# A two-layer diffusion step: four slices of a modulation sum move from TensorE to VectorE, and VectorE's sums get a new timetable

## What is computed

```python
def trunk_layer(l, x, cond, w_ada, b_ada, norm_pre, norm_post, w_in, w_out, ...):
    mod = jax.nn.silu(cond) @ w_ada[l] + b_ada[l]
    shift, scale, gate = jnp.split(mod[:, None, :], 3, axis=-1)
    h = rmsnorm(x, norm_pre[l]) * (1 + scale) + shift
    proj = h @ w_in[l]
    ...
    x = x + gate * rmsnorm(o @ w_out[l], norm_post[l])
    return x, k, v

for l in range(DEPTH):          # DEPTH = 2
    xp, kp, vp = trunk_layer(l, xp, c_ctx, ...)   # 128 context tokens
    xs, _, _ = trunk_layer(l, xs, c, ...)         # 256 latent tokens
```

## Time and profile before

| what | value |
|---|---|
| median of 3 runs | 1183.94 us (1182.51 to 1185.13) |
| the profiled execution: its own time | 1183.69 us |
| its span, first to last instruction | 1181.6 us |
| mean granted TensorE clock | 0.991 |
| PE busy | 1126.5 us, 95% |
| DVE busy | 715.6 us, 61% |

### The profile page before, as it was taken

How to read it: one execution, slowest core, us unless ns; L and a number is a source line. 1 busy time by engine, 2 the same in 40 slices (tenths; PEclk the granted TensorE clock), 3 DMA queues, 4 the chain that set the end, 5 groups by cost and what they waited for, 6 DMA issues and landing times.

```text
span 1181.6 us, 13864 instructions
## 1 busy us (share of the span) xinstructions
PE 1126.5 (95%) x5404; PEld 876.4 (74%) x5404; DVE 715.6 (61%) x985; ACT 421.4 (36%) x660; POOL 50.9 (4%) x98
## 2 busy tenths in 40 slices
PE   2999999999999999999999699999999999999996
PEld 1556667887787877788776588888878887878874
DVE  3445455788788785598873653567656764343335
ACT  4223234333455342233333762223323323243332
POOL 1000010000000001001101000000000000000000
PEclk9999999999999999999999899999999999999998
DMA  9999984565576567657767343455444654433413
GB/s 301 359 325 295 325 276 151 207 221 186 200 248 215 197 240 289 216 181 242 242 213 292 115 136 124 143 195 180 157 154 152 214 196 161 142 99 115 143 36 107
DMA packets 117857, 235.99 MB, mean 200 GB/s; under 512 B 5472, under 2 KB 42368, under 8 KB 114720
## 3 DMA queue, kind: packets, MB, share of 16 engines
q1 hardware_dynamic: 105776, 190.86, 47.7%
q0 software_dynamic: 11440, 41.08, 10.7%
q10 hardware_dynamic: 576, 3.16, 0.7%
HBM read 231.40 MB, written 3.67 MB: 199 GB/s over the span
## 4 chain that ended last, share of the span: by engine, by line
PE 81%; DVE 5%; DMA 5%; ACT 4%; issue 3%; SPq 2%; DVEq 0%; ACTq 0%
PE bank L814 23%; PE bank L816 23%; PE bank L815 23%; DMA raw_first<-in_w_ada 4%; DVE w_lo L1243 2%; PE bank L940 1%; SPq L615 1%; PE bank L752 1%; ACT w_hi L1022 1%; ACT silu L1087 1%; DVE x L1300 1%; PE bank L838 1%; PE bank L923 1%; PE bank L985 1%; PE bank L890 1%
## 5 line engine op out<-in xcount | busy, mean ns | idle before, releaser
L814 PE MATMUL bank<-w_hi,h_op 128*128 128x512 f32 x1128 | 464.7, 412 | 3.1 <-DVE w_lo L1243 2.6
L816 PE MATMUL bank<-w_hi,h_op 128*128 128x512 f32 x1128 | 443.8, 393 | 0.0
L815 PE MATMUL bank<-w_lo,h_op 128*128 128x512 f32 x1128 | 442.3, 392 | 0.0
L1243 DVE TENSOR_TENSOR w_lo<-raw,w_hi 128x1024 fp32r<-128x1024 f32 x224 | 273.1, 1220 | 182.8 <-ACT w_hi L1022 182.6
L1022 ACT ACTIVATE w_hi<-raw 128x1024 fp32r<-128x1024 f32 x224 | 234.2, 1053 | 214.0 <-PE bank L816 211.0
L814 PEld LDWEIGHTS bank<-w_hi,h_op 128*128 128x128 f32 x1128 | 213.2, 189 | 79.9 <-issue 35.3
L816 PEld LDWEIGHTS bank<-w_hi,h_op 128*128 128x128 f32 x1128 | 212.7, 189 | 46.9
L815 PEld LDWEIGHTS bank<-w_lo,h_op 128*128 128x128 f32 x1128 | 213.6, 189 | 39.8 <-issue 0.7
L1424 DVE SCALAR_TENSOR_TENSOR wide<-wide_raw,cond,wide 128x1024 f32<-128x1024 f32 x120 | 151.9, 1275 | 15.2 <-DMA wide_raw<-in_w_ada 15.1
L814 PE MATMUL bank<-w_hi,o_low 128*128 128x512 f32 x192 | 75.9, 396 | 0.0
L816 PE MATMUL bank<-w_hi,o_low 128*128 128x512 f32 x192 | 74.9, 390 | 0.0
(11 more groups left out here) (192 smaller groups left out, 797.3 us busy)
## 6 DMA issues: line engine op xcount, KB each, us to landing
raw<-in_w_in SPq DMA_DIRECT2D x68, 1024.0 KB, 6.1
raw_first<-in_w_ada SPq DMA_DIRECT2D x64, 512.0 KB, 7.6
raw<-in_w_ada SPq DMA_DIRECT2D x32, 1024.0 KB, 5.3
wide_raw<-in_w_ada POOLq DMA_DIRECT2D x64, 512.0 KB, 4.3
raw<-in_w_out SPq DMA_DIRECT2D x32, 1024.0 KB, 5.1
raw<-in_w_in SPq DMA_DIRECT2D x24, 512.0 KB, 6.8
x<-in_x_sample SPq DMA_DIRECT2D x2, 1024.0 KB, 9.7
x<-in_x_sample ACTq DMA_DIRECT2D x2, 1024.0 KB, 10.1
```

The source lines that it names most:

```text
L814: pe.matmul(out, operand(layer, kind, 0, k, t), hi, start=k == begin, stop=False)
L815: pe.matmul(out, operand(layer, kind, 0, k, t), lo, start=False, stop=False)
L816: last = pe.matmul(out, operand(layer, kind, 1, k, t), hi, start=False, stop=k == end)
L1243: dve.tensor_tensor(w_lo[:, half % WRING, :, :].rearrange("p k n -> p (k n)"), src, hi, ALU.subtract)\
```

## The change

Of the scale's 16 slices the first twelve stay on PE (six pairs, the last at step 123). The last four become 16 wide sums of DVE with four 512 KB load pairs of POOL, and a fold of their own, whose DVE part adds to `rows`. The gate's sums run at 11 steps for ten (steps 58 to 127, fold at 130), the scale's at one a step (131 to 146, fold at 149), the shift's at 9 steps for ten (150 to 206, fold at 209). The transpose of the scale's rows (`cols`) moves from step 165 to 168. POOL requests the scale's first two half slices ahead of its wait for the end of attention and of the DFT's constants.

```diff
-WIDE = [(GATE_BLOCK[0], FIRST, 10, 12, 10), (SHIFT_BLOCK, FIRST + 5, 13, 11, 10)]
+SCALE_ADA = 12
+
+WIDE = [(GATE_BLOCK[0], 0, FIRST, 10, 11, 10), (SCALE_BLOCK, SCALE_ADA, FIRST + 5, 3, 10, 10),
+        (SHIFT_BLOCK, 0, FIRST + 6, 6, 9, 10)]
...
-    pairs = [(m, k) for m in range(3) if m not in WIDE_BLOCKS for k in range(0, KT, 2)]
-    for n, (m, k) in enumerate(pairs):
-        put(FIRST, 5 + 14 * n, "ada", m, k, 2)
-    for m, c, s, step, per in WIDE:
-        for k in range(KT):
+    for n, k in enumerate(range(0, SCALE_ADA, 2)):
+        put(FIRST, 5 + 14 * n, "ada", SCALE_BLOCK, k, 2)
+    for m, k0, c, s, step, per in WIDE:
+        for k in range(k0, KT):
             for j in range(4):
-                put(c, s + step * (4 * k + j) // per, "wide_sum", m, k, j // 2, j % 2)
-        put(c, s + step * 4 * KT // per + 2, "wide_fold", m)
+                put(c, s + step * (4 * (k - k0) + j) // per, "wide_sum", m, k, j // 2, j % 2)
+        put(c, s + step * 4 * (KT - k0) // per + 2, "wide_fold", m)
...
-    put(10, 5, "cols", SCALE_BLOCK)
+    put(10, 8, "cols", SCALE_BLOCK)
...
             load_bias(GATE_BLOCK[0])
             load_wide(GATE_BLOCK[0])
+            load_wide(SCALE_BLOCK, 0, 2)
 
             wait_full(pool, "pv", len(units) - 1)
             pool.dma_start(dft_sb[:, :], dft).then_inc(dft_in, 16)
             load_weight(1)
             load_bias(SHIFT_BLOCK)
+            load_wide(SCALE_BLOCK, 2)
             load_wide(SHIFT_BLOCK)
...
+                    if m == SCALE_BLOCK:
+
+                        wait_free(dve, *ada_entry[m, SCALE_ADA - 1])
+                        other = rows
+                    else:
+                        dve.wait_ge(bias_in, 16 * (BIAS_ORDER.index(m) + 1))
...
+                    freed(dve.tensor_tensor(dst[:, :], side_bank(e)[:, :], other[:, :], ALU.add), e)
```

More of the change, by code:

```diff
@@ L81 @@
 FIRST = 3
-WIDE = [(GATE_BLOCK[0], FIRST, 10, 12, 10), (SHIFT_BLOCK, FIRST + 5, 13, 11, 10)]
+SCALE_ADA = 12
+WIDE = [(GATE_BLOCK[0], 0, FIRST, 10, 11, 10), (SCALE_BLOCK, SCALE_ADA, FIRST + 5, 3, 10, 10),
+        (SHIFT_BLOCK, 0, FIRST + 6, 6, 9, 10)]
 WIDE_BLOCKS = [w[0] for w in WIDE]
+WIDE_FROM = {w[0]: w[1] for w in WIDE}
+WIDE_LOADS = [(m, k, half) for m in WIDE_BLOCKS for k in range(WIDE_FROM[m], KT) for half in range(2)]
+NTH_WIDE = {x: n // 2 for n, x in enumerate(WIDE_LOADS)}
 BIAS_ORDER = [SCALE_BLOCK, GATE_BLOCK[0], SHIFT_BLOCK, GATE_BLOCK[1]]
@@ L550, in first_drain @@
         def first_drain(m):
-            return ("wide_fold", m) if m in WIDE_BLOCKS else ada_entry[m, 0]
+            return ada_entry[m, 0] if (m, 0) in ada_entry else ("wide_fold", m)
         def half_ahead(p):
@@ L673, in load_bias, with load_wide @@
                 pool.dma_start(bias_rows[:, :], ada_rows[m]).then_inc(bias_in, 16)
-            def load_wide(m):
+            def load_wide(m, first=0, last=2 * KT):
                 layer, third = BLOCKS[m]
-                for i in range(2 * KT):
+                k0 = WIDE_FROM[m]
+                for i in range(first, min(last, 2 * (KT - k0))):
                     if i >= 2:
@@ L683, in load_wide @@
                     else:
-                        pool.wait_ge(wide_summed[WIDE_BLOCKS[WIDE_BLOCKS.index(m) - 1]], 4 * KT - 2 + 2 * i)
-                    k, col = i // 2, third * D + LANES * (i % 2)
+                        prev = WIDE_BLOCKS[WIDE_BLOCKS.index(m) - 1]
+                        pool.wait_ge(wide_summed[prev], 4 * (KT - WIDE_FROM[prev]) - 2 + 2 * i)
+                    k, col = k0 + i // 2, third * D + LANES * (i % 2)
                     pool.dma_start(wide_raw[:, i % 2, :], w_ada[layer, k * P:(k + 1) * P, col:col + LANES])\
@@ L854, in side_product @@
                     pe.wait_ge(fold_in, 16)
-                    pe.wait_ge(wide_summed[e[1]], 4 * KT)
+                    pe.wait_ge(wide_summed[e[1]], 4 * (KT - WIDE_FROM[e[1]]))
                     for c_ in range(2):
@@ L872, in side_product @@
                     else:
-                        wait_free(pe, *(("wide_fold", e[1]) if e[1] in WIDE_BLOCKS else ada_entry[e[1], KT - 1]))
+                        wait_free(pe, "wide_fold", e[1])
                     for i in range(4):
@@ L1407, in part @@
                     m, k, half, c_ = e[1:]
-                    n = 4 * k + 2 * half + c_
+                    n = 4 * (k - WIDE_FROM[m]) + 2 * half + c_
                     cols = slice(LANES * half, LANES * (half + 1))
                     src = wide_raw[:, half, :]
-                    dve.wait_ge(wide_in[half], 16 * (KT * WIDE_BLOCKS.index(m) + k + 1))
+                    dve.wait_ge(wide_in[half], 16 * (NTH_WIDE[m, k, half] + 1))
                     if n == 0:
@@ L1430, in part @@
                     wait_full(dve, *e)
-                    dve.wait_ge(bias_in, 16 * (BIAS_ORDER.index(m) + 1))
-                    wait_full(dve, *{0: ("first_cols", len(STAGES) - 1), 2: ("cols", SCALE_BLOCK)}[m])
-                    freed(dve.tensor_tensor(dst[:, :], side_bank(e)[:, :], bias_rows[:, :], ALU.add), e)
+                    if m == SCALE_BLOCK:
[3 more added lines that the diff above has]
+                        dve.wait_ge(bias_in, 16 * (BIAS_ORDER.index(m) + 1))
+                        wait_full(dve, *{0: ("first_cols", len(STAGES) - 1), 2: ("cols", SCALE_BLOCK)}[m])
+                        other = bias_rows
+                    freed(dve.tensor_tensor(dst[:, :], side_bank(e)[:, :], other[:, :], ALU.add), e)
                     wait_free(dve, *e)
```

2 lines of the change are left out of this document (1 added, 1 removed).

## The result

The changed kernel is slower. Its median is 1189.51 us (1187.65 to 1191.04, four runs) against 1183.72 us (1182.51 to 1185.13) for the kernel before, run beside it. The ratio is 1.0045, with a 95% interval of 1.0032 to 1.0059. The predicted 1183.2 us is missed and so is the range, which ended at 1188.0. The profiled execution took 1187.65 us, the lowest of the four, with a span of 1185.9 us; all times within the trace are from that execution.

A forecast was written before the change was run, and what follows sets the result against it. The prediction took PE as the bound, with DVE close behind and its sums dependent on buffer return. It summed -2.04 - 1.08 + 0.7 + 1.9 = -0.5 us from 1183.69 to 1183.2 us, range 1180.3 to 1188.0.

The forecast's parts named there:

- pairs and fold: PE's side products: two scale pairs go, one fold comes, the other two folds only move; -2.04 us.
- the waits at 131 and 133: PE's waits for DVE's splits behind the transposes of these steps vanish; -1.08 us, ends 0 and -1.08.
- The fourth rival: The pairs were hidden, removing them saves nothing and the rest cancels: 1183.7 us; chance 0.03.
- the gate's pace: Attention stretch: the gate's faster sums fit into DVE's idle time; taken 0, upper end +6 us.
- the third rival: The gate's pace makes attention late, PE waiting before step 125, up to +6 us: 1189; chance 0.03.
- the scale's sums: Steps 131 to 146: buffer cycles 1.5 us late, DVE's margin taking about half; +0.7 us, ends 0 and +2.5.
- the shift's sums: Steps 150 to 206: buffers return slightly late at the faster pace; +1.9 us, ends 0 and +5.
- one sign of being wrong: Mean landing differing from 4.9 us by more than 0.4, or a wait in none of the named places.
- my own formula: Shift's buffer cycle: mean pair 3.04, request 0.29, landing 4.9, so 8.2 us against 7.65 that PE gives.
- margin that DVE wins back, 1 to 2 us: Shift's stretch: part of the buffers' 1.5 to 5 us lack goes into margin DVE regains where it does not wait.
- The second: Rival: DVE waits for transfers every cycle, PE for splits, steps 176 to 206: 1187.6 us; chance 0.22.
- The first rival: Buffers return in time, landing about 4.2 us; only PE's gain and the two waits count, -3.12: 1180.6; chance 0.26.

The follow-up runs named there:

- e1: The kernel before with only the gate's sums at the new pace, 11 steps for ten, fold at step 130: 1183.76 us.
- e3: The changed kernel with the shift's first three slices left out and its sums back at the old pace, 11 steps for ten: 1182.83 us.
- e4: The changed kernel with four buffers instead of two for the shift's loads, from load 10 (counted from 0) on: 1182.84 us, timed once.
- e5: The changed kernel without the shift's transfers after the first two; all its sums read those two half slices: 1183.66 us.
- e12: The changed kernel with four buffers for the shift, the kernel of e4, timed again in rounds: 1183.30 us, ratio 0.9983 to the kernel before.
- e13: The changed kernel once more, unaltered: 1189.13 us, ratio 1.0034 to the kernel before.
- e9: The changed kernel with the scale's 16 sums one step later (132 to 147, fold at 150), splits between pairs: 1187.63 us.
- e2: The kernel before with only the shift's sums at the new pace, 9 steps for ten from step 150: 1193.38 us.
- e11: e8 with the shift's even sums moved by one step, so each pair has a split inside: 1191.06 us, ratio 1.0047 to the kernel before.
- e8: e9 with 14 shift sums in steps 150 to 159, then one a step to 209, splits between pairs: 1181.62 us, ratio 0.9968 to the kernel before.
- e10: e8 with four buffers instead of two for the shift's loads from the tenth on: 1181.93 us, ratio 0.997 to the kernel before.

## Why the prediction was wrong

**Right: what the change takes from PE.** Predicted -2.04 for pairs and fold and -1.08 for the waits at 131 and 133. Measured -3.11 in the steps 130 to 137 and +0.04 in 148 to 159, together -3.07; e1 shows the waits apart, -1.16. The fourth rival (pairs hidden) is out. One step of the working was wrong and changed nothing: the gate's closing instructions (2.67 us) and the two sums that go (2.38) both stand ahead of the split of step 131, so by these numbers DVE is 0.3 us later there too, not 1.2 earlier; PE, 2 us later itself, did not have to wait.

**Nearly right: the gate's pace.** Predicted 0, measured +0.51 at step 114 (e1: +0.52). A wait of PE for an attention tile (`mixed`) is new there: the sign of the third rival came, at a tenth of its up to 6 us.

**Mis-sized: the scale's sums.** Predicted +0.7 (0 to +2.5), measured +1.61 (1.06 to 1.75 in e3, e4, e5, e12 and e13). The step named the cause, the split inside the pair, and e9 bears it out: moved by one step the term is -0.13. What was wrong was "of which DVE's margin takes about half": it took none. The two cycles of the slower buffer last 8.96 and 9.27 us (438.45 to 447.41 to 456.68) for 8.3, together 1.6 us too long, and 1.61 were lost.

**Failed: the shift's sums, "Taken: +1.9 us. Ends: 0 and +5".** Measured +5.63, and 6.30 in e13. Not the landing was longer than assumed; it was shorter, 4.3 us in the median and never over 4.9 where I had taken 4.9 on average (kernel after, loads of 540 to 610 us):

```profile
DMA to landing us min/median/max: 4.0/4.3/4.9
```

So one sign of being wrong came, a mean landing (4.3 too) off by more than 0.4 us, but on the side that should have cost less. By my own formula this landing gave 3.04 + 0.29 + 4.3 = 7.6 us of cycle for 7.65, so nothing lost. (With the 4.9 that it named, the formula gave 5 us less 1 to 2, so 3 to 4; the +1.9 was nearer to the lower end of the range, and the sum does not say why.)

What failed is the step from mean values to "the cycle is 8.2 us and PE gives it 7.65". Neither the pairs nor the steps are even. At nine steps for ten sums four pairs in ten have a split inside (I had taken half), and they come in a row: every pair from step 169 to 176 and from 187 to 194, none from 177 to 186. And a buffer's next use stands four steps later as a rule, but three where two sums share a step. Take the buffer that is used at the steps 168, 171, 175 and 178. In the kernel before, these ten steps take 22.2 us. The three cycles, even with 0.29 and 4.3 us each, take 2.5 + 3.6 + 3.6 + 3 x 4.6 = 23.5: too long by 1.3 us. The next two cycles, from 178 to 186, take 14.1 for 16.3. The mean fits and the worst run does not. Measured were 26.0 us for the ten steps, from 527.54 to 553.55. The other 2.5 are a drain inside a pair (0.6), landings of 4.5, 4.9 and 4.5 us (0.9), and one request that POOL made 1.24 us behind the sum instead of 0.29 (0.95; the profile names nothing that it waited for):

```profile
527.54 2.47 DVE L1433 SCALAR_TENSOR_TENSOR wide<-wide_raw,cond,wide 128x1024 f32<-128x1024 f32 x2
...
531.25 0.53 POOL L693 DMA_DIRECT2D wide_raw<-in_w_ada  x1 [4.28 <-issue]
...
535.73 1.28 DVE L1433 SCALAR_TENSOR_TENSOR wide<-wide_raw,cond,wide 128x1024 f32<-128x1024 f32 x1 [1.55 <-DMA wide_raw<-in_w_ada]
```

DVE thus waited 1.55 and 1.67 us, at 535.73 and 544.54, and met the double sum and the three drains from 546.88 on late. The run that follows, without splits in the pairs, does not repay PE, since a step that PE began late stays late. The timeline says so: the splits for the steps 172, 174, 178, 180 and 182 end 0.05 us before the step begins, and only then the margin grows again, to 2.4 us at step 188, in time for the next run of bad pairs. The "margin that DVE wins back, 1 to 2 us" was counted as a gain and was only a return to the start.

What is shown and what is not: that the loss comes through the time until a buffer is back, and not from the traffic or from DVE's work alone, is shown by e4, e5 and e12 (nothing lost with the same work of DVE). That DVE must also be nearly full is shown by the kernel before and e3, which waited 6.9 and 4.9 us and lost nothing. e2 and e3 show that the pace of the shift, not the moved slices, brings it in. That the place of the split matters is shown at one sum a step, by e9 and by e11 against e8, in both with landings that changed along. At nine steps for ten sums no run moved the splits alone, so how the 5.63 us divide between split, double sums and landings is worked out from one trace, not shown.

**The rivals.** The second came true in its mechanism and nearly in its time (1187.6 against 1187.65 for the profiled execution, 1189.5 for the median), chunks 11 and 12 at 36.7 and 36.1 us, "36 us and more". That the time agrees so well is luck: the profiled execution was the lowest of four, and the stretches outside the change happened to cancel. But its condition, "a mean landing of some 5.1 us", was false: the loss came with 4.3. I judged its chance by the mean landing, and gave 0.22. The first rival did rest on landings of 4.2 us, which came, and was wrong all the same. The Trainium skill's figure, "DMA: Bandwidth & Descriptors", section "Anatomy of one DMA — SWDGE (gpsimd) path", works out to an estimate of 3.2 us for 512 KB, and here too no landing of that stretch was under 4.0.

**Outside the change.** The seam (+1.27) and the steps 304 to 307 (-1.66) follow the granted clock, below. They nearly cancel.

## What to carry over

A buffer that comes back late must be judged at the worst run of its cycles, not at the mean one: write down for each buffer what stands on the in-order engine between its first and last use, and count every instruction of other work in it as turnaround. Where a sum of two instructions holds a buffer, place both on the same side of the foreign instruction; here that, with the sums spread evenly (e8), left nothing for two extra buffers to win (e10), and it cost nothing. A mean busy share that fits (33 of 34 us) leaves no room for waits: waits that cost nothing beside 27.6 and 30.3 us of work cost 5 us beside 33.

## What the runs showed of the hardware

**A load of POOL lands later when it is asked for just behind a 1 MB weight load of SP.** In e11 twelve loads from 508 to 616 us were requested 1.5 to 2.1 us behind such a load and took 4.4 to 6.6 us, 5.6 on average; the eleven others took 3.9 to 5.1, 4.4 on average. Three views of e11: SP's request, then POOL's 1.5 us behind it with its landing; then the next one of POOL, 5.3 us behind:

```profile
556.16 0.37 SPq L655 DMA_DIRECT2D raw<-in_w_out  x1
```

```profile
L695 POOL DMA_DIRECT2D wide_raw<-in_w_ada x1: 528/528/528, 557.6 to 557.6; - x1
...
DMA to landing us min/median/max: 5.8/5.8/5.8
```

```profile
L695 POOL DMA_DIRECT2D wide_raw<-in_w_ada x1: 528/528/528, 561.5 to 561.5; - x1
...
DMA to landing us min/median/max: 4.6/4.6/4.6
```

The kernel after has the same sign in a smaller size: five loads requested 1.5 to 2.1 us behind such a load from 497 to 608 us took 4.5 to 5.0 us, 4.8 on average, the 22 others 4.0 to 4.7, 4.2 on average. And the longest landing of the earlier trace rows, 7.7 us, was requested 6.2 us behind one. So the distance is not the whole of it; no experiment moved SP's loads alone.

**The clock at the steps 305 to 307 differs between kernels that do the same there.** Windows of the kernel before and of e1 (column before the DMA share: granted clock in parts of 2.4 GHz), which differ in the gate's pace 430 us earlier:

```profile
856.00:866.00 10.00, 7.95 (x35) 5.13 (x34) 3.17 (x5) 2.61 (x5) 0.00 (x0) 1.00 0.28 94
866.00:869.50 3.50, 3.50 (x10) 2.67 (x10) 3.50 (x5) 0.96 (x2) 0.00 (x0) 0.51 0.84 287
```

```profile
856.00:866.00 10.00, 8.50 (x38) 5.56 (x36) 1.40 (x2) 2.98 (x4) 0.00 (x0) 1.00 0.42 159
866.00:869.50 3.50, 2.95 (x13) 2.42 (x14) 3.50 (x6) 1.55 (x2) 0.00 (x0) 1.00 0.53 131
```

Before, the clock stands at 0.51 (1.2 GHz) behind a pause of PE, 2.05 us of waiting for a split of DVE, in e1 at 1.00 (2.4 GHz) behind the same one, 2.05 us long too. It is worth 1.6 us. It fell there in four of the fourteen traces (before, e3, e4, e5) and in ten not, e12 with the very kernel of e4 among these. What decides it stays open.
